# Side stages of a two-layer decoder step weighted anew, a store wait moved by one stage, and head groups regrouped

## The chip, the cores and the metric

The kernel runs on one core of one Trainium2 chip. The core has a matrix engine (PE, with its weight loads as PEld), a vector engine (DVE), a scalar engine (ACT), a general engine (POOL) and a sync engine (SP), and 16 DMA engines that move data between the chip's memory (HBM) and the on-chip SBUF. The metric is the device time of one execution in microseconds (us).

## The reference

It is one inference step of a decoder trunk with two layers, for a prompt of 256 tokens and 32 new tokens of eight running sequences ("samples"), 1024 wide, all in float32. Each layer has a mixer and then a PEER expert layer, each followed by `x <- LayerNorm(ALPHA * x + sublayer(x))`.

```
layer 0 mixer   HGRN2 recurrence (8 heads) beside sparse attention (8 query heads, 2 kv heads)
layer 1 mixer   q, k, v = x @ w_in (1024 x 3072), rotated; 16 heads of dilated attention,
                samples also over 256 cached positions each; o @ w_out (1024 x 1024)
expert layer    q = x @ w_q (1024 x 2048); scores against 2 x 128 sub-keys per head, 8 heads;
                top 16 of each half, top 16 of their sums -> 128 experts per token, softmax gate
                y = sum over the 128 of  gate * gelu(u[e] . x) * v[e]
```

Outputs are the new x of prompt and samples and the new cache rows, among them keys and values of layer 1 (`dil_p`, `dil_s`).

## The kernel before, in words

The tokens lie in three tiles: prompt tiles 0 and 1 of 128 tokens, and tile 2 with the 32 samples. The first mixer and the routing of tile 2 run alone, until about 650 us. Then one long block runs both expert layers as 576 **steps** (class `Experts`). A visit is one layer's experts for one tile; the visits are, in this order, layer 0 tiles 2, 0, 1 and layer 1 tiles 0, 1, 2, with 32, 128, 128, 128, 128 and 32 steps (`VISITS`, `FIRST`; four experts of each sample share a step). Step s does this:

- POOL fetches for each of the 128 partitions one expert row (u and v side by side, 8 KB) by an indirect DMA into a slot of the ring `uv`, which has 8 slots (L1802). It waits until step s - 8 has released the slot.
- DVE multiplies u with x and sums (`dot`, L1820). ACT makes gelu and the weight, and spreads the weight on a diagonal (L1866, L1875, L1888).
- PE adds diagonal times v into two banks of PSUM (L1912, three steps later), four matmul instructions a row. For steps that `by_dve` names, DVE does it instead: `acc += w * v` (L1834). `by_dve(s)` is true where s modulo 4 is in the third entry of the window in `WINDOWS` that holds s. At the end of a visit PE adds `acc` to its sum (L1919), and DVE forms the norm.

Beside the steps run **side stages**: the routing of the tile that comes next, and the layer 1 mixer of each tile. `WINDOWS` gives for each list of side stages the step at which it begins. A prompt tile's list (`dilated_tile`) is: transposes of x; the projection to q, k and v (`project_wide`, 12 weight pieces of 1 MB through 3 slots); `rotate_and_store` on DVE; `turn_qk` (transposes of q and k on PE); attention; output projection and norm; transposes; then the projection of the routing queries. The samples' list is split in two: `samples_first_part` runs in the window "samples" with head groups 0 and 1, `samples_second_part` in "mixer 2" with groups 2 and 3. A head group (`dilated_sample`) transposes 2 MB of cached keys, forms scores and sums 2 MB of cached values; SP fetches them by 16 DMAs of 256 KB, the first group's during the stage before it, the next group's keys and values when the group before has read its own.

Each engine runs one program. A stage is cut in ticks with a weight each, and `both` deals the ticks of a window to its steps so that the share of weight done follows the share of steps done. At the end of each stage the three engines drain and add to a semaphore `ended`; SP adds its own (L2015) after it has issued the stage's DMAs and the next stage's early loads, and nobody goes on before all four are there (L1948, L1951, L2018). A stage's end is thus a barrier for the expert steps too. `rotate_and_store` (L1445) ends on SP's side with a wait for all stores so far (`wait_for_stores`), and this keeps SP from adding.

```
weights = [0.5] * 2 + [w for st in stages for w in st.weights + [0.5] * 2] if stages else []
...
next(main)
while done < len(weights) and (n == b - a - 1 or reached[done] * (b - a) <= reached[-1] * (n + 1)):
    next(side)
    done += 1
```

Of the kernel before, what the change touches and what calls it, by code (L numbers as in the profile page):

```python
# [326 lines left out]
def transposes(k, name, groups, banks=ALL_BANKS, loads=(), early=False, after=(), by=("vector", "scalar")):  # L327

    nc, nb = k.nc, len(banks)
    turned, v_out, s_out, loaded = [k.sem(name, n) for n in ("turned", "v_out", "s_out", "loaded")]
    ident, n_by = k.c("ident"), len(by)
    stage = Stage(k, len(groups) + 1, 1.5)
    stage.read = [(turned, len(groups))]
    sizes = [(srcs[0].shape[0], int(np.prod(srcs[0].shape[1:]))) for srcs, _ in groups]
    copies = {"vector": (v_out, nc.vector.tensor_copy), "scalar": (s_out, nc.scalar.copy)}
    outs = [copies[engine] for engine in by]
    stage.done = [(outs[side][0], len(range(side, len(groups), n_by))) for side in range(n_by)]

    def out_view(i):
        (rows, width), (srcs, dst) = sizes[i], groups[i]
        flat = k.bank(banks[i % nb])[0:width, 0:rows * len(srcs)]
        if len(dst.shape) == 3:
            return flat.rearrange("p (a b) -> p a b", b=dst.shape[2])
        return flat

    @stage.on("early loads" if early else "sync")
    def _(sp):
        for dst, src in loads:  # L350
            sp.dma_start(dst, src).then_inc(loaded, 16)

    @stage.on("tensor")
    def _(pe):
        if loads:
            pe.wait_ge(loaded, 16 * len(loads))
        wait_all(pe, after)
        for i, (srcs, dst) in enumerate(groups):
            rows, width = sizes[i]
            j = i - nb  # L360
            if j >= 0:
                pe.wait_ge(outs[j % n_by][0], j // n_by + 1)
            for n, src in enumerate(srcs):
                last = nc.tensor.transpose(k.bank(banks[i % nb])[0:width, n * rows:(n + 1) * rows], src, ident[0:rows, 0:rows])
            last.then_inc(turned, 1)
            yield
        yield

    def take_out(eng, side):
        done, copy = outs[side]  # L370
        yield
        for i in range(len(groups)):
            if i % n_by == side:
                eng.wait_ge(turned, i + 1)
                copy(groups[i][1], out_view(i)).then_inc(done, 1)  # L375
            yield

    for side, engine in enumerate(by):
        stage.on(engine)(lambda eng, side=side: take_out(eng, side))
    return stage  # L380
# [83 lines left out]
def project_wide(k, name, w, groups, out, wbuf, t, banks, after=(), by=("vector", "scalar"), resident=False):  # L464
# [19 lines left out]
    for at, base, n_j, done in ends:  # L484
        for j in range(n_j):
            spot = min(at + j // 2, len(ticks) - 1)
            ticks[spot].append(("leave", base + j, done))
    stage = Stage(k, len(ticks), 1.0)
    n_by = len(by)
    copies = {"vector": (v_out, nc.vector.tensor_copy), "scalar": (s_out, nc.scalar.copy)}  # L490
    outs = [copies[engine] for engine in by]
# [143 lines left out]
def project_out_and_norm(k, name, catT, w_piece, gain, bias, w, gb, z, stats, tiles=(0, 1, 2), banks=ALL_BANKS, before_loads=(),  # L635
# [5 lines left out]
    row_landed, used, variance, rooted, normed = [k.sem(name, n) for n in ("rows_landed", "w_used", "variance", "rooted", "normed")]  # L641
    n_t, pieces = len(tiles), KC // 2
    per = [len(w_piece(i, w[:, 0])) for i in range(pieces)]
    stage = Stage(k, pieces * n_t * 2 + 3 * n_t, 1.2)
    stage.weights[pieces * n_t * 2:] = [3.5] * (3 * n_t)
    stage.tile_done = [[(normed, n + 1)] for n in range(n_t)]
    stage.rows_in = rows_in or (row_landed, 32)

# [96 lines left out]
def attention(k, name, items, bufs, pairs=(0, 2), turn_banks=(4, 5), before_scores=(), before_values=()):  # L745
# [18 lines left out]

    ticks = []

    def scores(i):
        if i < n_items:
            count = len(items[i]["scores"])
            for at in range(0, count, 3):  # L770
                ticks.append([("scores", i, at, min(at + 3, count))])
# [8 lines left out]
    for i in range(n_items):  # L780
# [9 lines left out]
                    ticks[-1] = [("turn", r + 1), ("copy", r + 1)] + ticks[-1]  # L790
        ticks.append([("leave", i)])
    stage = Stage(k, len(ticks), 1.0)
    stage.read = [(summed, len(rounds))]

    def view(i):
# [646 lines left out]
def rotate_and_store(k, name, qk, val, tiles, out_p, out_s, tmp):  # L1442

    nc = k.nc
    rotated = k.sem(name, "rotated")  # L1445
    stage = Stage(k, 4 * len(tiles), 2.5)

    @stage.on("vector")
    def _(dve):
        for n, t in enumerate(tiles):  # L1450
            r = ROWS[t]
            for at in (0, 512, 1024, 1536):
                rotate(k, qk[0:r, n, at:at + 512], qk[0:r, n, at:at + 512], (t, r), HEADS // 2, tmp)
                if at == 1536:
                    nc.vector.memset(k.pad[:, :], 0.0).then_inc(rotated, 1)
                yield

    @stage.on("sync")
    def _(sp):
        for n, t in enumerate(tiles):  # L1460
            sp.wait_ge(rotated, n + 1)
            dst = out_s[0].rearrange("b t x h d -> (b t) x (h d)") if t == 2 else \
                out_p[0, 0, 128 * t:128 * (t + 1)].rearrange("p x h d -> p x (h d)")
            k.store(sp, dst[:, 0, :], qk[0:ROWS[t], n, D:2 * D])
            k.store(sp, dst[:, 1, :], val[0:ROWS[t], t, :])
        k.wait_for_stores(sp)
    return stage


# [95 lines left out]
def route(k, name, layer, t, qT, keysT, slots, gate, xs, ctx, bank0, routed=None, own=None, after=()):  # L1565
# [26 lines left out]
    weights += [0.5, 0.5]  # L1592
    TICKS = len(weights)
    stage = Stage(k, TICKS, 1.0)
    stage.weights = weights

    def copy_out(copy, b):
        return copy(s[0:r, 4 * b:4 * b + 8].rearrange("p a b -> p (a b)"),
# [126 lines left out]
WINDOWS = (  # L1725
    ("route 0 0", FIRST[0], ()),
    ("route 0 1", FIRST[1] - 6, ()),
    ("samples", FIRST[1] + 42, (3,)),
    ("mixer 0", FIRST[2] + 6, (3,)),
    ("route 1 0", FIRST[3] - 48, ()),  # L1730
    ("nothing", FIRST[3] - 10, (3,)),
    ("mixer 1", FIRST[3] + 6, (3,)),
    ("route 1 1", FIRST[4] - 48, ()),
    ("mixer 2", FIRST[4] - 10, (3,)),
    ("route 1 2", FIRST[5] - 48, ()),
# [219 lines left out]
def experts_and_side_work(k, experts, windows):  # L1955

    ended = k.sem("side_stage_ended")
    spans = []
    for i in range(len(windows)):
        spans.append((windows[i][0], windows[i + 1][0] if i + 1 < len(windows) else experts.ticks))  # L1960

    def both(name, eng):
        main = {"tensor": experts.tensor, "vector": experts.vector, "scalar": experts.scalar}[name](eng)
        base = 0
        for (a, b), (_, stages) in zip(spans, windows):
            side = side_ticks(k, stages, name, eng, ended, base) if stages else iter(())
            weights = [0.5] * 2 + [w for st in stages for w in st.weights + [0.5] * 2] if stages else []
            base += len(stages) + 1 if stages else 0
            reached = np.cumsum(weights)
            done = 0  # L1970
            for n in range(b - a):
# [4 lines that stand above are left out]
            for _ in side:  # L1976
                raise AssertionError("side work left over")
        for _ in main:
            raise AssertionError("steps left over")

    with k.nc.Block() as block:
        @block.gpsimd
        def _(pool):
            experts.pool(pool)

        @block.tensor
        def _(pe):
            both("tensor", pe)

        @block.vector  # L1990
        def _(dve):
            both("vector", dve)

        @block.scalar
        def _(act):
            both("scalar", act)

        @block.sync
        def _(sp):
            experts.load_rows(sp, 0)  # L2000
            n, layer = 0, 1
            for start, stages in windows:
                if not stages:
                    continue
                if layer < DEPTH and start > FIRST[layer * TILES] + LAG + 2:
                    experts.load_rows(sp, layer)
                    layer += 1
                chain = [Stage(k, 0)] + stages
                for stage, following in zip(chain, stages + [None]):
                    if "sync" in stage.parts:  # L2010
                        stage.parts["sync"](sp)
                    if following and "early loads" in following.parts:
                        following.parts["early loads"](sp)
                    n += 1
                    sp.sem_inc(ended, 1)  # L2015
                    sp.wait_ge(ended, 4 * n)
                    for sem in stage.sems:
                        sp.sem_clear(sem)  # L2018
            experts.stores(sp)
# [36 lines left out]
def turn_qk(k, name, t, qk, qT, kT):  # L2056

    groups = [([qk[0:ROWS[t], 0, at + 128 * (c + j):at + 128 * (c + j + 1)] for j in range(4)], dst[:, c:c + 4, cols(t)])
              for dst, at in ((qT, 0), (kT, D)) for c in range(0, HP, 4)]
    return transposes(k, name + "_qk", groups, SIDE_BANKS)  # L2060


def mix_out(k, name, t, a, w, ctx, before_loads=()):
# [20 lines left out]
def samples_first_part(k, name, a, o, val, kT, qT, wbuf, cached):  # L2084
# [9 lines left out]
            stages.append(rotate_and_store(k, name + "_rot", qk, val, (2,), o["dil_p"], o["dil_s"], tmp))  # L2094
        stages.append(turn_qk(k, name, 2, qk, qT, kT))
    with ExitStack() as outer:
        stages += sample_groups(k, name, (0, 1), a, qT, kT, val, cached, outer)
    return stages


def samples_second_part(k, name, a, val, kT, qT, cached):
# [1 line left out]


    with ExitStack() as outer:
        stages = sample_groups(k, name, (2, 3), a, qT, kT, val, cached, outer)
        w = cached[:, 0].rearrange("p b n (c z) -> p (b n c) z", z=256).rearrange("p (s c n) z -> p s c (n z)", s=2, c=2)
        stages.append(mix_out(k, name, 2, a, w, outer, stages[-1].stages[0].read))
    stages.append(transpose_x(k, name + "_y", (2,), SIDE_BANKS))
# [174 lines left out]
```

## Time and profile before

| what | value |
|---|---|
| median of 3 runs | 2496.88 us (2495.08 to 2505.72) |
| profiled execution | 2510.64 us, its span 2508.9 us |
| mean granted PE clock | 0.856 of full speed |
| bytes moved | 750.84 MB, mean 299 GB/s |

The page gives for each engine its busy time as a share of the span, then the span in 40 equal slices (62.7 us each) with one digit per slice. The busy table of the trace gives the same for any stretch: length, then busy time and instruction count of PE, PEld, DVE, ACT and POOL, then the granted PE clock, the mean busy share of the 16 DMA engines, and GB/s. A share can read a little over 1, as transfers overlap at the edges. In lists of instructions the bracket gives how long the engine had been idle and what released it.

### The profile page before, as it was taken

What the parts mean: (1) busy time and instruction counts of PE and PEld (TensorE: products, weight loads), DVE (VectorE), ACT (ScalarE), POOL (GpSimd) and SP (SyncE); (2) the same over time, 40 slices, a digit from 0 to 9 for tenths busy, and PEclk for the clock granted to TensorE, in tenths of its full rate; (3) what the DMA queues carried; (4) which work ended last, traced back from release to release, by engine and by line L of the source; (5) the groups of instructions that cost most, each with busy time, mean ns of one, the idle gap of its engine ahead of it and who ended that gap; (6) DMA issues with size and microseconds to landing.
All of it is one profiled execution on the core that took longest, in us unless ns stands there. A gap on an engine that the chain in (4) does not pass through costs nothing. (4 is left out here: it accounts for less than half of the span.)

```text
span 2508.9 us, 19125 instructions
## 1 busy us (share of the span) xinstructions
PE 1942.4 (77%) x5651; PEld 886.6 (35%) x5651; DVE 1458.8 (58%) x3327; ACT 570.5 (23%) x1755; POOL 702.9 (28%) x612
## 2 busy tenths in 40 slices
PE   8968288899567797679867877767798687888675
PEld 3356155534213322344323432323343244323221
DVE  0043633138599846565376498548649766547975
ACT  0010122101223312222143223215222232212222
POOL 4000000000234523333133344323334333334442
PEclk9986556698789998887989998888899888899988
DMA  8300120300689999998989999987999999899997
GB/s 279 94 17 1 38 68 0 141 27 1 253 297 386 422 420 400 396 389 348 394 342 387 422 419 387 415 339 311 351 421 420 360 369 398 341 414 421 405 385 297
DMA packets 144945, 750.84 MB, mean 299 GB/s; under 512 B 22077, under 2 KB 46537, under 8 KB 63817
## 3 DMA queue, kind: packets, MB, share of 16 engines
q0 software_dynamic: 84480, 608.21, 60.1%
q1 hardware_dynamic: 60360, 141.41, 15.3%
q8 instruction: 45, 0.74, 0.1%
q14 instruction: 60, 0.48, 0.1%
HBM read 743.96 MB, written 5.60 MB: 299 GB/s over the span
## 5 line engine op out<-in xcount | busy, mean ns | idle before, releaser
L1912 PE MATMUL ps<-uv,diag 128*128 128x512 f32 (+1 forms) x1908 | 1013.6, 672 | 318.0 <-ACT diag L1888 206.7
L1802 POOL DMA_INDIRECT uv<-in_experts_dram,slots x576 | 672.3, 1167 | 1743.1 <-PE ps L1912 1051.8
L1820 DVE CUSTOM_DVE_ANT_0 uv<-uv,x 128x1024 f32<-128x1024 f32 x512 | 621.8, 1226 | 430.5 <-DMA uv<-in_experts_dram,slots 345.7
L1912 PEld LDWEIGHTS ps<-uv,diag 128*128 128x128 f32 (+1 forms) x1908 | 358.4, 201 | 876.5 <-issue 557.7
L1866 ACT ACTIVATE gelu<-dot 128x2 f32<-128x2 f32 x288 | 58.6, 203 | 1066.3 <-DVE dot L1820 1066.1
L1888 ACT ACTIVATE diag<-const,wgt 128x128 f32<-128x128 f32 (+1 forms) x477 | 166.5, 386 | 9.4
L1875 ACT ACTIVATE wgt<-gate,gelu 128x1 f32<-128x1 f32 x576 | 138.0, 287 | 68.0 <-PEq L1948 31.6
L1834 DVE SCALAR_TENSOR_TENSOR acc<-uv,wgt,acc 128x1024 f32<-128x1024 f32 x94 | 120.4, 1281 | 0.8 <-ACT wgt L1875 0.8
L441 PE MATMUL ps<-even_w,xT 128*128 128x512 f32 (+3 forms) x240 | 100.2, 570 | 6.6 <-issue 5.3
L1820 DVE CUSTOM_DVE_ANT_0 uv<-uv,xs 128x1024 f32<-128x1024 f32 x64 | 78.1, 1225 | 44.0 <-DMA uv<-in_experts_dram,slots 41.3
L524 PE MATMUL ps<-uv,xT 128*128 128x512 f32 (+1 forms) x192 | 85.9, 609 | 1.8 <-ACT xT L375 1.8
L524 PE MATMUL ps<-last_w,xT 128*128 128x512 f32 x160 | 76.3, 621 | 12.1 <-DMA last_w<-in_odd_w_in_dram 11.7
L524 PE MATMUL ps<-first_w,xT 128*128 128x512 f32 x160 | 73.1, 599 | 12.2 <-DMA first_w<-in_odd_w_in_dram 10.6
L441 PEld LDWEIGHTS ps<-even_w,xT 128*128 128x128 f32 (+1 forms) x240 | 38.1, 165 | 68.3 <-issue 64.2
L456 DVE COPY h<-ps 128x512 f32<-128x512 f32 (+3 forms) x8 | 5.0, 627 | 91.2 <-PE ps L441 51.6
L524 PEld LDWEIGHTS ps<-uv,xT 128*128 128x128 f32 (+1 forms) x192 | 32.2, 169 | 53.6 <-issue 51.1
L524 PEld LDWEIGHTS ps<-last_w,xT 128*128 128x128 f32 x160 | 31.0, 197 | 54.3 <-issue 36.2
L524 PEld LDWEIGHTS ps<-first_w,xT 128*128 128x128 f32 x160 | 29.6, 190 | 53.8 <-issue 33.2
L879 DVE TENSOR_TENSOR q_rows<-ps,const 128x512 f32<-128x512 f32 (+3 forms) x16 | 10.2, 640 | 63.7 <-PE ps L824 63.7
L1820 DVE DVE_READ_ACCUMULATOR2_ANT dot<- 128x1 f32 x576 | 47.2, 82 | 0.0
L524 PE MATMUL ps<-sample_w_in,xT 128*32 128x512 f32 x96 | 44.4, 596 | 2.7 <-DMA sample_w_in<-in_odd_w_in_dram 2.6
L1062 PE MATMUL ps<-hT,hg_key 64*128 64x128 f32 (+1 forms) x304 | 24.7, 317 | 22.4 <-PEq L1008 13.2
(430 smaller groups left out, 1930.8 us busy)
## 6 DMA issues: line engine op xcount, KB each, us to landing
sample_cache<-in_cache_dil_kv_dram SPq DMA_DIRECT2D x64, 256.0 KB
sample_w_in<-in_odd_w_in_dram SPq DMA_DIRECT2D x12, 1024.0 KB
first_w<-in_odd_w_in_dram SPq DMA_DIRECT2D x12, 1024.0 KB
last_w<-in_odd_w_in_dram SPq DMA_DIRECT2D x12, 1024.0 KB, 10.7
uv<-in_experts_dram,slots POOLq DMA_INDIRECT x576
even_w<-in_even_w_in_dram SPq DMA_DIRECT2D x8, 1024.0 KB, 8.4
uv<-in_peer_w_q_dram SPq DMA_DIRECT2D x8, 1024.0 KB, 13.9
first_w<-in_peer_w_q_dram SPq DMA_DIRECT2D x8, 1024.0 KB, 10.4
```

Source lines behind the costliest of these rows:

```text
L441: last = nc.tensor.matmul(k.bank(banks[i % nb])[0:ROWS[t], 0:widths[j]], k.xT[:, 4 * half + c, cols(t)], wbuf[:, load % slots, c, 0:widths ...
L456: copy(out(j, t), k.bank(banks[i % nb])[0:ROWS[t], 0:widths[j]]).then_inc(done, 1)
L524: last = nc.tensor.matmul(k.bank(banks[job])[0:r, :], k.xT[:, chunk, cols(t)], wbuf[:, i % slots, width * c + 512 * j:width * c + 512 * (j ...
L879: step(nc.vector.tensor_tensor(view(i), sc, bc(it["mask"], 1, g), ALU.add))
L1062: last = nc.tensor.matmul(dst, key[p, hd // 2, cols(t)], pT[p, hd // 2, cols(t)], start=True, stop=True, skip_group_check=True)
L1802: self.k.nc.gpsimd.indirect_dma_start(out=self.uv[:, s % RING, :], out_offset=None, in_=self.table, in_offset=bass.IndirectOffsetOnAxis(ap ...
L1820: ins = nc.vector.tensor_tensor_reduce(self.uv[:, s % RING, 0:D], self.uv[:, s % RING, 0:D], x, 1.0, 0.0, ALU.mult, ALU.add, self.dot[:, g ...
L1834: nc.vector.scalar_tensor_tensor(self.acc[:, :], v, w, self.acc[:, :], ALU.mult, ALU.add).then_inc(self.added, 1)
L1866: nc.scalar.activation(self.gelu[:, grp % 2, :], self.dot[:, grp % 2, :], ACT.Gelu).then_inc(self.gelued, 1)
L1875: ins = nc.scalar.activation(self.wgt[:, grp % 2, g:g + 1], self.gate[:, t, j:j + 1], ACT.Copy, scale=self.gelu[:, grp % 2, g:g + 1])
L1888: last = nc.scalar.activation(self.diag[:, step % RING, 0:w], k.c(shape), ACT.Copy, scale=self.wgt[:, grp % 2, g:g + 1])
L1912: last = nc.tensor.matmul(k.bank(c)[0:m, :], self.diag[:, s % RING, 0:m], self.uv[:, s % RING, D + 512 * c:D + 512 * (c + 1)], start=(j == ...
```

## The change

It does six things. The weights of the ticks are set anew: transposes 0.9 for 1.5, projection 1.9 for 1.0 (its last tick 0.8), output projection 1.9 for 1.2 and its three norm ticks 3.6, 1.6 and 3.1 for 3.5 each, rotation 3.0 for 2.5, route ticks times 2.5 (alone in their windows, so only their ratio to the ends of stages changes), ends of stages 0.3 for 0.5 (two ticks each). Attention ticks get a weight each from a function of what the tick does. The wait for the stores moves from the rotation to the stage after it, `turn_qk`, ahead of that stage's early loads. Head group 2 moves from "mixer 2" to "samples". The window "samples" begins 4 steps earlier. In the windows "samples", "mixer 0" and "mixer 1" DVE adds every second row and not every fourth.

```diff
@@ transposes
-    stage = Stage(k, len(groups) + 1, 1.5)
+    stage = Stage(k, len(groups) + 1, 0.9)
@@ project_wide
-    stage = Stage(k, len(ticks), 1.0)
+    stage = Stage(k, len(ticks), 1.9)
+    stage.weights[-1] = 0.8
@@ project_out_and_norm
-    stage = Stage(k, pieces * n_t * 2 + 3 * n_t, 1.2)
-    stage.weights[pieces * n_t * 2:] = [3.5] * (3 * n_t)
+    stage = Stage(k, pieces * n_t * 2 + 3 * n_t, 1.9)
+    stage.weights[pieces * n_t * 2:] = [3.6, 1.6, 3.1] * n_t
@@ attention
+    def work(tick):
+        pe = dve = 0.2
+        for what, at, *some in tick:
+            it = items[rounds[at][0] if what in ("turn", "copy", "values") else at]
+            sweep = it["groups"] * it["n"] / 840
+            if what == "scores":
+                pe += 0.4 * (some[1] - some[0])
+            elif what == "turn":
+                pe += 0.2 * it["groups"]
+            elif what == "values":
+                pe += (0.36 if it["groups"] == 1 else 0.18) * (some[1] - some[0])
+            elif what == "mask":
+                dve += 2 * sweep
+            elif what == "normalise":
+                dve += (1 if it["count"] is None else 3) * sweep + 0.2
+            elif what == "leave":
+                dve += 0.2
+        return max(pe, 1.2 * dve)
...
     stage = Stage(k, len(ticks), 1.0)
+    stage.weights = [work(tick) for tick in ticks]
@@ rotate_and_store
-    stage = Stage(k, 4 * len(tiles), 2.5)
+    stage = Stage(k, 4 * len(tiles), 3.0)
...
-        k.wait_for_stores(sp)
     return stage
@@ route
-    stage.weights = weights
+    stage.weights = [2.5 * w for w in weights]
@@ WINDOWS
-    ("samples", FIRST[1] + 42, (3,)),
-    ("mixer 0", FIRST[2] + 6, (3,)),
+    ("samples", FIRST[1] + 38, (1, 3)),
+    ("mixer 0", FIRST[2] + 6, (1, 3)),
...
-    ("mixer 1", FIRST[3] + 6, (3,)),
+    ("mixer 1", FIRST[3] + 6, (1, 3)),
@@ experts_and_side_work
-            weights = [0.5] * 2 + [w for st in stages for w in st.weights + [0.5] * 2] if stages else []
+            weights = [0.3] * 2 + [w for st in stages for w in st.weights + [0.3] * 2] if stages else []
@@ turn_qk
-    return transposes(k, name + "_qk", groups, SIDE_BANKS)
+    stage = transposes(k, name + "_qk", groups, SIDE_BANKS)
+
+    @stage.on("sync")
+    def _(sp):
+        k.wait_for_stores(sp)
+    return stage
@@ samples_first_part
-        stages += sample_groups(k, name, (0, 1), a, qT, kT, val, cached, outer)
+        stages += sample_groups(k, name, (0, 1, 2), a, qT, kT, val, cached, outer)
@@ samples_second_part
-        stages = sample_groups(k, name, (2, 3), a, qT, kT, val, cached, outer)
+        stages = sample_groups(k, name, (3,), a, qT, kT, val, cached, outer)
```

## Rows read from the trace of the kernel before

**Rows 1.** Page, part 1: busy time of each engine, share of the span, instructions.
```profile
PE 1942.4 (77%) x5651; PEld 886.6 (35%) x5651; DVE 1458.8 (58%) x3327; ACT 570.5 (23%) x1755; POOL 702.9 (28%) x612
```
**Rows 2.** Page, part 2: DMA busy tenths and GB/s in 40 slices.
```profile
DMA  8300120300689999998989999987999999899997
GB/s 279 94 17 1 38 68 0 141 27 1 253 297 386 422 420 400 396 389 348 394 342 387 422 419 387 415 339 311 351 421 420 360 369 398 341 414 421 405 385 297
```
**Rows 3.** Page, part 3: DMA queues with packets, MB, share of 16 engines.
```profile
q0 software_dynamic: 84480, 608.21, 60.1%
q1 hardware_dynamic: 60360, 141.41, 15.3%
```
**Rows 4.** Busy table, last stretch without side work.
```profile
2389.00:2492.00 103.00, 72.02 (x131) 19.53 (x132) 67.65 (x103) 26.66 (x97) 45.39 (x38) 0.85 0.97 397
```
**Rows 5.** Busy table: two head groups; mixer 0 projection, rotation, turning, attention.
```profile
1019.50:1097.30 77.80, 60.08 (x219) 31.21 (x219) 45.69 (x75) 20.91 (x67) 28.02 (x25) 0.87 1.01 399
1097.30:1173.50 76.20, 71.45 (x223) 38.79 (x223) 51.49 (x85) 23.27 (x68) 28.36 (x24) 0.79 0.88 350
1182.90:1252.60 69.70, 58.41 (x132) 24.49 (x132) 21.59 (x32) 10.21 (x34) 14.33 (x14) 1.00 0.97 398
1252.60:1277.20 24.60, 9.11 (x20) 3.63 (x20) 16.96 (x38) 3.55 (x13) 6.79 (x6) 0.79 0.84 328
1277.20:1286.10 8.90, 8.62 (x28) 4.44 (x28) 7.15 (x11) 3.63 (x11) 3.97 (x3) 0.83 0.39 133
1286.10:1332.70 46.60, 35.01 (x125) 15.62 (x125) 40.23 (x72) 27.24 (x64) 18.40 (x15) 0.85 1.01 417
```
**Rows 6.** Busy table: mixer 1 projection to attention; mixer 2 groups, output projection.
```profile
1595.20:1670.90 75.70, 62.25 (x132) 26.19 (x132) 21.23 (x32) 9.99 (x34) 13.12 (x14) 0.91 0.93 376
1670.90:1695.10 24.20, 9.20 (x16) 3.37 (x16) 15.80 (x36) 2.67 (x10) 6.23 (x5) 0.68 0.89 327
1695.10:1705.30 10.20, 10.05 (x29) 5.29 (x30) 7.83 (x12) 3.52 (x11) 3.08 (x4) 0.75 0.44 148
1705.30:1772.50 67.20, 46.51 (x180) 22.58 (x178) 51.59 (x74) 31.51 (x71) 21.02 (x17) 0.82 0.84 329
1994.30:2068.30 74.00, 65.58 (x216) 36.00 (x217) 48.40 (x81) 22.28 (x63) 24.44 (x22) 0.80 0.96 362
2068.30:2141.70 73.40, 60.65 (x211) 31.54 (x210) 39.76 (x67) 19.15 (x60) 24.83 (x23) 0.85 0.94 374
2141.70:2190.30 48.60, 37.02 (x76) 11.54 (x76) 29.20 (x44) 12.30 (x38) 18.00 (x16) 0.89 0.92 356
```
**Rows 7.** Instructions in order of time, end of mixer 0's rotation (start, length, instruction).
```profile
1270.02 0.36 SPq L177 DMA_DIRECT2D out_dil_p_dram<-first_qk  x1
...
1277.31 3.44 PE L1912 MATMUL ps<-uv,diag 128*128 128x512 f32 x4 [13.57 <-SPq L2018]
1277.35 1.23 DVE L1820 CUSTOM_DVE_ANT_0 uv<-uv,x 128x1024 f32<-128x1024 f32 x1 [7.35 <-SPq L2018]
```
**Rows 8.** Groups of DVE instructions by line, mixer 1 attention: busy, mean ns.
```profile
L1820 DVE CUSTOM_DVE_ANT_0 uv<-uv,x 128x1024 f32<-128x1024 f32 x17 | 20.2, 1222 | 0.4 <-ACT gelu L1866 0.2
L1834 DVE SCALAR_TENSOR_TENSOR acc<-uv,wgt,acc 128x1024 f32<-128x1024 f32 x4 | 5.1, 1280 | 0.0
```
**Rows 9.** Instructions in order of time, PE, end of mixer 0's projection.
```profile
1241.22 3.70 PE L524 MATMUL ps<-first_w,xT 128*128 128x512 f32 x8 [1.79 <-DMA first_w<-in_odd_w_in_dram]
1244.76 1.88 PE L1912 MATMUL ps<-uv,diag 128*128 128x512 f32 x4
```
**Rows 10.** Instructions in order of time, SP's cache loads in the samples window.
```profile
992.38 5.18 SPq L351 DMA_DIRECT2D sample_cache<-in_cache_dil_kv_dram  x8
997.60 21.78 SPq L1525 DMA_DIRECT2D sample_cache<-in_cache_dil_kv_dram  x8
1041.18 16.21 SPq L351 DMA_DIRECT2D sample_cache<-in_cache_dil_kv_dram  x8
```
**Rows 11.** Busy table of SP's filter, the steps stopped behind cache loads: clock, DMA, GB/s.
```profile
1990.00:2000.00 10.00, 0.50 1.03 330
```

## The prediction

> **What bounds the kernel now.** I read the page's engine shares and slices first, then the DMA queues, then the busy table stage by stage, then the instructions in order of time at the stage ends. On the whole span nothing looks full: PE 77%, DVE 58% [rows 1]. The slices tell more: from the 14th on, when the expert steps run, the DMA engines are nine tenths busy nearly everywhere, and where they are, they move 420 to 422 GB/s [rows 2]. The rows that the expert steps fetch are 608 of 751 MB [rows 3]. One step fetches 128 x 8 KB = 1.05 MB; at 421 GB/s that is 2.49 us. The stretch without side work that ends the kernel has DMA at 0.97 with PE and DVE at 0.70 and 0.66 of its 103 us [rows 4]. So the time of the 576 steps is bytes over 421 GB/s plus what the DMA engines stand idle. The change moves no byte: it can only take idle DMA time away or add some.
>
> Where is that idle time? One minus the DMA share, times the length, from the busy table: last head group of the samples window 9.1 us; mixer 0, projection 2.1, rotation 3.9, turning 5.4; mixer 1, projection 5.3, rotation 2.7, turning 5.7, attention 10.8; mixer 2, head groups 3.0 and 4.4, output projection 3.9 [rows 5, 6]. Together 56 us. (A full stretch reads 1.01, so this is a little low.)
>
> **The change, part by part.** A stage gets its share of its window's steps by weight. I worked the weight lists out with both sets of numbers; the old ones give 16.7 steps for mixer 1's attention, where the trace has 17 dots [rows 8]. Steps before -> after: samples projection 20.8 -> 25.4, rotation 8.8 -> 6.8, turning 6.8 -> 2.8, head group 25.2 -> 19.7 (and there are three). Mixer 0: projection 13.5 -> 20.0, rotation and turning 10.1 -> 7.6, attention 15.0 -> 15.2, output 10.9 -> 10.3. Mixer 1: projection 13.1 -> 17.8, rotation and turning 9.9 -> 6.7, attention 16.7 -> 21.7, output 10.7 -> 9.1. Mixer 2: one head group of 30.8 steps for two of 22.6, output 15.1 -> 20.4. The steps whose row DVE adds up rise from 99 to 160 (every second instead of every fourth in three windows).
>
> *The store wait.* At the end of each rotation SP waits until the keys and values are stored before it lets the three engines on. In mixer 0 it issued the stores at 1270.0 and PE and DVE ran again at 1277.3: DVE had waited 7.35 us, PE 13.57 [rows 7]. PE stood still, released no ring slot, and the DMA share fell to 0.84 and 0.39. Moved behind the turning (2 to 3 steps, some 6 us), the wait is nearly over when SP comes to it. Gone: 3.9 + 5.4 + 2.7 + 5.7 = 17.7 us. In the samples window DMA was not idle there, so nothing is counted. What is late next is DVE. Mixer 0, 7.6 steps: 7.6 dots x 1.22, 3.8 additions x 1.28 [rows 8] and the stage's own 16.96 - 6 x 1.22 - 1.28 = 8.4, with about 1.0 of copies, make 23.6 us, against 7.6 x 2.49 + 2.5 for the stores = 21.4 us of DMA. Mixer 1 by the same sum: 21.9 against 19.2. Left idle: 5. Net -12.7.
>
> *The projections.* Eight projection matmuls take 3.54 us from start to start at the granted clock of 1.00, so one is 0.44 and a step's row (four) 1.77 [rows 9]. In mixer 0 after: 96 x 0.44 + 10 x 1.77 = 60 us of PE, against (20.0 x 1.05 + 12.6)/0.421 = 80 us of DMA. PE no longer follows weights that have just landed. The 2.1 + 5.3 us go but for 0.5: -6.9.
>
> *The attention.* In mixer 1 DVE was busy 51.6 of 67.2 us (77%); 17 dots and 4 additions are 25.8, so the attention itself is 25.8. After: 21.7 x 1.22 + 10.9 x 1.28 + 25.8 = 66 us, against 21.7 x 2.49 + 7.5 (three weight pieces) = 61.5 of DMA. DVE bounds this stage. At 90% busy it takes 73.5, 12 over; the ring of eight rows takes up some 3 of it. I keep 9 of the old 10.8: -1.8. In mixer 0 the same sum gives 43.8 of DVE against 45.3, at 90% 3.4 over: +2. Bounds: none over, and 24.7 over in mixer 1 if DVE stays at 77%.
>
> *The third head group.* A group after: PE 60.1 us at clock 0.87 is 52 at full clock, 19 rows x 1.77 of it the steps' own, so 19 of its own [rows 5]; with 9.9 rows on PE 36 us, against (19.7 x 1.05 + 4.2)/0.421 = 59 of DMA. It fits. The last group still ends where the visit ends; I keep 5 of 9.1: -4.1. Mixer 2 loses a group and has room: 11.3 -> 1.3, -10.0.
>
> *The rest* (transposes at 0.9, norm ticks, the 0.3 around a stage, the route window) moves ticks by less than two steps between stages where DMA already reads about 1.01 [rows 5]: 0, bounds -3 and +3.
>
> Sum: -12.7 - 6.9 - 1.8 + 2 - 4.1 - 10.0 = -33.5. The profiled execution took 2510.6 (span 2508.9 and 1.7 around it), so 2477 in its terms; it ran 13.8 above the median of the runs. Against 2496.9 I forecast 2463.
>
> **Rivals.** *DVE is the new bound.* DVE takes 61 more additions, 61 x 1.28 = 78 us. If its stages keep their old busy share (77% in mixer 1, 86% in mixer 0), attention gives 24.7 and 5.5 over, and rotation with turning 9.2 each, which eats the store gain: -6.9 - 10.0 - 4.1 + 0.7 + 13.9 + 5.5 = -0.9, 2496. For it: DVE waited in mixer 1 though not full. Against: more steps per tick are more room between its waits.
>
> *All idle time goes*: -56, 2441. For it: each stage but two fits with room. Against: the end of a visit has idle time that no weight removes.
>
> *SP is held by its queue* (slower). In the samples window SP issues 16 cache loads during the turning, after the change behind the store wait. With the queue empty eight issues took 5.18 us, 0.65 each; the next eight took 21.78, and a later eight 16.21 [rows 10]: if four and five of them were quick, the others took 4.8 and 4.3 each. In 2.8 steps they don't fit: the engines wait at the stage's end. If 11 of the 16 took 5 us, the stage would take 5 x 0.5 + 55 + 5 = 62 us, while the DMA engines have 16 x 0.26 + 8 x 1.05 = 12.6 MB, 30 us: 32 idle, and 8 more at each of two group ends: 48 - 33.5 = +14.5, 2511. Against: with the rows stopped the loads alone kept DMA at 1.03 and 330 GB/s [rows 11], so the queue drains when the ring is full. It decides if that speed is not reached. The Trainium skill (DMA: Bandwidth & Descriptors, Queues, rings and completion order) says that an engine takes turns between queues packet by packet; the small cache packets then get a small share beside 8 KB rows and the full one without them, which the two issue rates here agree with.
>
> *The PE clock falls* (slower). With fewer rows PE idles more. The granted clock was 1.00 where PE was busy 58.4 of 69.7 us and 0.68 to 0.87 in the patchier stages, and a row's four matmuls took 3.44 us at the low level against 1.88 [rows 5 to 7, 9]. If groups and output projections ran wholly at 1.2 GHz: a group 72 us of PE against 59, 13 x 3 = 39 over; outputs (32 x 0.44 + 5.2 x 1.77 = 23 at full clock, 22 in mixer 1) 46 against 31 and 44 against 28, 31 over: 70 - 33.5 = +36.5, 2533. It decides when their clock goes below about 0.65; it was 0.79 to 0.99. The Trainium skill (TensorE: Matmul & The Clock Gate, HAM oscillation) warns of just this, PE gaps behind DMA waits throttling each burst; the row after the 13.57 us gap, at the low level, agrees.
>
> **How the numbers follow.** Forecast 0.55 (2450 to 2480), all idle gone 0.12, DVE bound 0.18, SP 0.08, clock 0.07. Half a per cent is 12.5 us, about what this kernel's measurement can tell. Faster: 0.67 and 0.03 of the DVE case, 0.70. Same: 0.13 of DVE's, 0.03 of SP's, 0.01 of the clock's, 0.17. Slower: 0.13. The range leaves out SP's and the clock's cases and the extreme of full removal: 2436 to 2503.
>
> **What would show it.** The rotation-to-turning passage of mixers 0 and 1 at DMA 0.9 or more, with PE and DVE not released by SP; projections at 1.00; the DVE wait for rows present in the group stages; attention of mixer 1 with DVE 0.85 to 0.95 busy. It is wrong if the DMA share of attention falls below 0.8, if SP's 16 issues in the samples window leave DMA below 0.9, or if PEclk there is under 0.7.

## The result and the profile after

| | before | after |
|---|---|---|
| median of the runs | 2495.98 us (4 runs) | 2470.78 us (4 runs, 2458.0 to 2471.85) |
| ratio | 1 | 0.9879, 95% interval 0.9838 to 0.992 |
| profiled execution | 2510.64 us, span 2508.9 | 2469.82 us, span 2468.0 |
| mean granted PE clock | 0.856 | 0.841 |

The forecast was 2463 us, 33.5 us less than before, in a range of 2436 to 2503. The medians lie 25 us apart and the means 30 (2498.0 and 2467.9); the ratio stands for 30 us less (20 to 40). All ratios below leave out executions in the chip's slower state, one of which, of the kernel "rows to DVE only, PE's matmuls put back", took 4597 us. First the page of the kernel after, parts 1 and 2 as in [rows 1, 2].

```profile
PE 1848.0 (75%) x5407; PEld 851.8 (35%) x5407; DVE 1529.8 (62%) x3388; ACT 553.8 (22%) x1694; POOL 721.3 (29%) x612
DMA  8300120300588999999999999999899999999997
GB/s 282 97 18 1 38 69 0 135 35 1 211 334 344 421 420 392 356 370 375 415 403 373 405 415 420 404 413 359 312 369 412 420 373 419 411 421 421 416 382 304
```

PE lost 94 us of busy time and DVE gained 71: the 61 additions of 1.28 us are 78, and the rest of DVE's work took 7 less. Neither says where time was won. The DMA line does: from the 14th to the 39th slice five digits were under 9 before, and one is after. The bytes are the same (750.8 MB).

Now the busy table of the kernel after by stage (length; busy time of PE, PEld, DVE, ACT, POOL; clock, DMA share, GB/s). In order: the samples' turning and three head groups; mixer 0's projection, rotation, turning, attention.

```profile
976.30:1000.20 23.90, 9.21 (x24) 4.20 (x24) 6.54 (x10) 1.60 (x7) 3.75 (x4) 0.57 0.93 336
1000.20:1066.80 66.60, 51.78 (x179) 31.36 (x179) 41.65 (x66) 15.93 (x49) 21.16 (x18) 0.68 0.94 346
1066.80:1131.30 64.50, 46.02 (x183) 26.03 (x183) 42.95 (x68) 16.31 (x50) 24.27 (x20) 0.79 1.01 392
1131.30:1187.80 56.50, 45.55 (x187) 26.04 (x187) 47.09 (x76) 18.53 (x50) 19.99 (x20) 0.89 0.95 368
1195.00:1270.50 75.50, 64.37 (x136) 26.94 (x136) 38.28 (x53) 12.29 (x43) 22.74 (x22) 0.93 1.01 419
1270.50:1289.00 18.50, 10.69 (x12) 3.22 (x12) 17.81 (x38) 3.06 (x11) 5.94 (x5) 0.63 1.01 399
1289.00:1301.80 12.80, 5.35 (x20) 4.03 (x20) 6.40 (x10) 2.46 (x7) 3.52 (x3) 0.78 0.98 355
1301.80:1347.40 45.60, 28.18 (x108) 13.60 (x108) 42.35 (x73) 25.78 (x59) 15.23 (x14) 0.80 0.98 380
```

Mixer 1's projection, rotation, turning, attention and output projection; mixer 2's head group and output projection.

```profile
1593.40:1674.40 81.00, 64.38 (x136) 26.79 (x136) 34.73 (x48) 11.20 (x39) 18.32 (x18) 0.94 1.00 408
1674.40:1691.70 17.30, 4.41 (x8) 1.36 (x8) 16.68 (x36) 3.06 (x11) 6.56 (x6) 0.71 0.86 321
1691.70:1699.30 7.60, 5.48 (x20) 3.69 (x20) 5.45 (x9) 2.14 (x6) 2.11 (x2) 0.75 0.76 263
1699.30:1776.10 76.80, 48.72 (x172) 23.44 (x172) 64.92 (x89) 31.96 (x73) 24.16 (x22) 0.76 0.86 340
1776.10:1811.30 35.20, 22.82 (x48) 9.53 (x48) 21.74 (x32) 7.99 (x22) 11.18 (x10) 0.91 0.88 346
1986.80:2070.50 83.70, 71.57 (x243) 35.95 (x243) 60.78 (x99) 27.00 (x81) 38.96 (x31) 0.93 0.99 394
2070.50:2130.40 59.90, 44.39 (x92) 14.15 (x92) 36.63 (x55) 14.96 (x48) 24.16 (x21) 0.94 1.01 416
```

Read with one minus the DMA share, times the length, as in the prediction:

| idle DMA time, us | before | forecast | after |
|---|---|---|---|
| rotation and turning, mixers 0 and 1 | 17.7 | 5 | 4.5 |
| projections, mixers 0 and 1 | 7.4 | 0.5 | 0 |
| mixer 1 attention | 10.8 | 9 | 10.8 |
| mixer 0 attention | 0 | 2 | 0.9 |
| head groups of the samples window | 9.1 | 5 | 6.8 |
| mixer 2, groups and output projection | 11.3 | 1.3 | 0.8 |
| not in the forecast: mixer 1 output projection (1776.1) | 0.3 | - | 4.2 |
| not in the forecast: samples' turning | 0.5 | - | 1.7 |

(Before, the samples' turning, 992.4 to 1019.5 us, had DMA at 0.98.) The forecast stages fall from 56.3 to 23.8 us, 32.5 less, against 33.5 forecast; the two at the bottom take 5.1 back, which leaves 27.4. The two spans lie 41 us apart, but 4.5 of it lies ahead of the first fetch of the expert steps (650.7 and 646.2 us), in a part that the change doesn't touch, and the profiled execution before was above the median by 14 us, so I don't count all of it as the change's.

### The profile page after: what moved, and what is told of

Same layout as the page of the kernel before. It is cut to its first block, busy times and chain, and to the rows that moved or that the text cites. A ratio compares the mean times of both kernels' runs of the same rounds, so it can differ in the third digit from the quotient of the medians.

```text
span 2468.0 us, 18705 instructions
## 1 busy us (share of the span) xinstructions
PE 1848.0 (75%) x5407; PEld 851.8 (35%) x5407; DVE 1529.8 (62%) x3388; ACT 553.8 (22%) x1694; POOL 721.3 (29%) x612
## 4 chain that ended last, share of the span: by engine, by line
DMA 22%; DVE 20%; PE 18%; issue 5%; SPq 1%; ACT 1%; POOL 1%; PEldq 1%; DVEq 1%; PEld 0%; ACTq 0%
DMA uv<-in_experts_dram,slots 14%; PE ps L1933 9%; DVE uv L1841 7%; PE ps L525 4%; DVE acc L1855 2%; DMA last_w<-in_odd_w_in_dram 2%; DMA first_w<-in_odd_w_in_dram 2%; PE ps L846 1%; PE ps L685 1%; SPq L1546 1%; PE ps L874 1%; DVE route_s L1675 1%; DMA out_dil_p_dram<-dil_val 1%; DMA last_w<-in_peer_w_q_dram 1%; DMA sample_rows<-in_peer_sub_keys_dram 1%
## 5 line engine op out<-in xcount | busy, mean ns | idle before, releaser
L1823 POOL DMA_INDIRECT uv<-in_experts_dram,slots x576 | 690.7, 1199 | 1685.2 <-PE ps L1933 923.2
L1933 PE MATMUL ps<-uv,diag 128*128 128x512 f32 (+1 forms) x1664 | 897.1, 681 | 286.5 <-ACT diag L1909 222.1
L1933 PEld LDWEIGHTS ps<-uv,diag 128*128 128x128 f32 (+1 forms) x1664 | 314.2, 202 | 783.4 <-issue 446.7
L1855 DVE SCALAR_TENSOR_TENSOR acc<-uv,wgt,acc 128x1024 f32<-128x1024 f32 x155 | 198.4, 1280 | 2.0 <-ACT wgt L1896 2.0
L1909 ACT ACTIVATE diag<-const,wgt 128x128 f32<-128x128 f32 (+1 forms) x416 | 148.7, 386 | 9.4
L685 PE MATMUL ps<-even_w_out,xT 128*128 128x512 f32 (+1 forms) x96 | 42.8, 607 | 0.0
## 6 DMA issues: line engine op xcount, KB each, us to landing
uv<-in_peer_w_q_dram SPq DMA_DIRECT2D x8, 1024.0 KB, 13.9
```

Of the source, the lines that this page charges most:

```text
L685: last = nc.tensor.matmul(bank(n, h)[0:ROWS[t], :], catT[:, 2 * i + c, cols(t)], w[:, i % slots, c, 512 * h:512 * (h + 1)], start=(i == 0 ...
L1823: self.k.nc.gpsimd.indirect_dma_start(out=self.uv[:, s % RING, :], out_offset=None, in_=self.table, in_offset=bass.IndirectOffsetOnAxis(ap ...
L1855: nc.vector.scalar_tensor_tensor(self.acc[:, :], v, w, self.acc[:, :], ALU.mult, ALU.add).then_inc(self.added, 1)
L1909: last = nc.scalar.activation(self.diag[:, step % RING, 0:w], k.c(shape), ACT.Copy, scale=self.wgt[:, grp % 2, g:g + 1])
L1933: last = nc.tensor.matmul(k.bank(c)[0:m, :], self.diag[:, s % RING, 0:m], self.uv[:, s % RING, D + 512 * c:D + 512 * (c + 1)], start=(j == ...
```

## The experiments

All ratios are to the kernel before, which ran beside the kernel tested on the same chip. There were three such sets of four kernels, each on a chip of its own, in the order of the table. The medians of the kernel before were 2495.2, 2496.9 and 2490.6 us, and two ratios of one set compare better than two of different sets. They are told in the order in which they answer.

| kernel | ratio | interval |
|---|---|---|
| store wait moved, nothing else | 0.9959 | 0.9923 to 0.9996 |
| weights only | 0.9934 | 0.9908 to 0.996 |
| rows to DVE only | 1.0048 | 1.0018 to 1.0077 |
| regrouping only | 1.0025 | 0.9997 to 1.0053 |
| after, store wait put back | 0.9925 | 0.9898 to 0.9953 |
| after, DVE rows as before | 0.9859 | 0.9818 to 0.9901 |
| after, groups two and two | 0.9899 | 0.9872 to 0.9926 |
| after, store wait later still | 0.9877 | 0.9848 to 0.9906 |
| rows to DVE only, PE's matmuls put back | 1.0027 | 1.0 to 1.0055 |
| after, PE's matmuls put back | 0.9976 | 0.9949 to 1.0002 |
| after, wait later, DVE rows as before | 0.9893 | 0.9852 to 0.9934 |
| after, wait later, DVE rows as before in mixer 1 | 0.9872 | 0.9837 to 0.9907 |

**The store wait, alone and taken back.**

```diff
 def rotate_and_store        # store_only: before with
-        k.wait_for_stores(sp)
 def turn_qk                 # the wait as its "sync" part
+        k.wait_for_stores(sp)
```

> The kernel before with only the store wait moved from the rotation to the turning stage. Theory (the time is bytes over 421 GB/s plus idle DMA time, and the wait costs what DMA idles in rotation and turning of the two prompt mixers): 17.7 us of idle there, some 4 stay because DVE is a little over in the rotation, so about -13 us, ratio 0.995; in the samples window nothing, since DMA was busy there. Rival (the ring makes up for the wait later): within 3 us of before. Rival (SP is held: the cache loads of the samples window now stand behind the stores): slower by up to 5 us, and the engines wait longer than 9 us at the end of the samples' turning.

> The kernel after with the store wait back at the end of the rotation. Theory: as in the kernel before, rotation and turning of both prompt mixers idle the DMA engines for some 18 us where the kernel after has 4: about 12 us slower than the kernel after, ratio to the kernel before 0.993. Rival (the turning of the kernel after is too short to hide the wait, as its engines still waited 6.3 us there in mixer 0): 5 us slower than after at most, 0.990.

Alone it is worth 0.41%, 10 us; taken out of the kernel after it costs 0.46%, 11.5 us, though the intervals of those two overlap and they come from different sets. The theory said 13 and 12. The busy table of the first, mixer 0's rotation and turning, then mixer 1's, and of the second, the same four stages:

```profile
1240.90:1259.20 18.30, 10.81 (x20) 4.22 (x20) 16.94 (x38) 3.55 (x13) 6.69 (x6) 0.82 0.95 370
1259.20:1268.30 9.10, 8.88 (x28) 4.44 (x28) 7.15 (x11) 3.64 (x11) 3.97 (x3) 0.80 0.92 339
1653.10:1670.30 17.20, 9.19 (x16) 3.37 (x16) 15.78 (x36) 2.67 (x10) 6.24 (x5) 0.76 0.97 364
1670.30:1680.80 10.50, 10.27 (x29) 5.34 (x30) 7.86 (x12) 3.53 (x11) 3.12 (x4) 0.74 0.83 304
```

```profile
1257.70:1283.80 26.10, 7.91 (x12) 2.32 (x12) 19.42 (x40) 3.25 (x12) 7.97 (x7) 0.69 1.01 418
1283.80:1289.90 6.10, 5.65 (x20) 4.19 (x20) 4.77 (x7) 2.26 (x6) 0.06 (x1) 0.66 0.07 28
1667.80:1693.80 26.00, 5.57 (x8) 1.85 (x8) 17.17 (x37) 3.06 (x11) 6.07 (x6) 0.68 0.82 300
1693.80:1700.10 6.30, 5.48 (x20) 3.69 (x20) 3.92 (x6) 1.26 (x3) 0.94 (x1) 0.70 0.00 0
```

With the wait the rotation lasts 24 to 26 us, and in the kernel after the turning behind it has next to no DMA (0.07 and 0.00): the rows asked for had landed while the engines stood still, and POOL asked for the next one only when PE had released a slot, 10.8 and 15.7 us after its last request. Without the wait the rotation lasts 17 to 18 us and DMA stays at 0.83 or more. So in these stages the ring doesn't make up for the wait. As a whole the interval of the first run still reaches 0.9996, within the 3 us of that rival; it is the table that speaks against it. The third theory, SP held in the samples window, came in part: at the end of the samples' turning PE now waited 17.7 us for 13.9, but with DMA at 1.03, so it cost nothing that shows.

**The weights alone.** The kernel after with the wait, the third entries and the groups as before.

> The kernel after with the store wait, the third entries of the windows and the head groups as before, so that only the weights of the ticks are new. Theory: the projections' 7.4 us of idle time go, mixer 2's output projection has 3.9 of which 2 go, the attention gets more steps but DVE has one row in four only, so 4 of its 10.8 go; the turning is shorter, which leaves the store wait as it was: about -13 us, ratio 0.995. Rival (the weights only shift the idle time from stage to stage): within 4 us of before.

Measured 0.9934, 16.5 us, the largest gain of the four parts. The reverse, the kernel after with the old weights, was not run. Its busy table: mixer 0's projection, mixer 1's attention, mixer 2's output projection.

```profile
1163.30:1242.00 78.70, 70.10 (x156) 29.71 (x156) 32.37 (x48) 13.73 (x48) 23.49 (x21) 0.98 1.01 419
1693.10:1763.70 70.60, 49.84 (x196) 23.56 (x194) 60.47 (x86) 34.20 (x81) 25.77 (x22) 0.90 0.95 369
2117.00:2165.60 48.60, 37.89 (x76) 10.96 (x76) 29.23 (x44) 11.73 (x36) 19.73 (x16) 0.89 1.01 411
```

Against [rows 5, 6] DMA goes from 0.97 to 1.01, from 0.84 to 0.95 and from 0.92 to 1.01. The attention lasts 3.4 us longer and takes five steps more.

**The rows alone, and with PE's load put back.**

```diff
-    ("samples", FIRST[1] + 42, (3,)),        # rows_only: before with (1, 3) in three windows
+    ("samples", FIRST[1] + 42, (1, 3)),
...
+                elif s % 4 == 1:             # rows_warm: in Experts.tensor, zeros x constant
+                    for c in range(2):
+                        nc.tensor.matmul(k.bank(c)[0:m, :], self.zero[:, 0:m], k.const[:, 0:512], start=False, stop=False,
+                                         skip_group_check=True)
```

> The kernel before with only the third entries of the windows samples, mixer 0 and mixer 1 set to (1, 3), so that DVE adds every second row there. Theory: PE sets the pace at the ends of the projections (idle 2.1 and 5.3 us), in part of mixer 1's attention and in the last head group (9.1); half of that goes, about -9 us, ratio 0.996. Rival (DVE is the new bound): mixer 1's attention gains DVE work of 4 x 1.28 = 5 us and the rotations 3 in all, which cancels it: 0. Rival (the PE clock falls with fewer rows): clock in the head groups from 0.87 and 0.79 to under 0.7 and the time up by 5 us or more.

> rows_only with PE's load put back without DVE's taken away: for the rows that moved to DVE (steps with s modulo 4 = 1) PE adds a tile of zeros times a constant tile, so PE issues the same matmuls as the kernel before and DVE the same additions as rows_only. If the loss of rows_only (1.0048) comes from the PE clock, which fell from 0.99 to 0.87 and 0.85 in the two output projections, the clock comes back and this is as fast as before, 1.000, the output projections at 3 us of excess over their bytes, not 6. If it comes from DVE's additions, this stays at 1.005. If PE's relief was worth something all the same, it is slower than both, 1.008.

My theory of 9 us gained was wrong: the part is a loss, 1.0048. The output projections of mixers 0 and 1 tell of the clock. In the busy table, as they were before, where [rows 5, 6] left them out:

```profile
1332.70:1370.10 37.40, 28.45 (x64) 11.75 (x64) 21.93 (x33) 9.07 (x26) 15.73 (x12) 0.99 0.98 386
1772.50:1806.60 34.10, 28.53 (x64) 11.83 (x64) 22.99 (x35) 9.17 (x27) 16.02 (x12) 0.99 0.99 382
```

With the rows alone:

```profile
1322.60:1363.80 41.20, 26.05 (x52) 10.54 (x52) 25.16 (x37) 8.20 (x23) 14.86 (x12) 0.87 0.93 361
1765.30:1805.30 40.00, 28.90 (x56) 11.59 (x56) 26.64 (x38) 8.29 (x24) 13.87 (x13) 0.85 0.90 353
```

With PE's matmuls put back:

```profile
1327.80:1366.10 38.30, 30.00 (x64) 12.10 (x64) 24.18 (x35) 8.20 (x23) 15.40 (x12) 0.95 0.89 348
1775.60:1814.30 38.70, 30.23 (x64) 12.42 (x64) 26.47 (x38) 8.29 (x24) 15.25 (x12) 0.93 0.93 360
```

In mixer 1 PE has 8 matmuls fewer than before (56 for 64) and is busy as long (28.90 against 28.53): what the rows gave, the clock took, 0.85 for 0.99. Put back, the clock rises to 0.93 to 0.95, the DMA share doesn't. As a whole 1.0027 lies between the two theories, and its interval touches 1.0 and overlaps that of the rows alone (from another set). What can be said: with the weights of before, the extra matmuls on PE cost nothing that can be measured, so taking them off was worth nothing measurable. In the two output projections the clock came back and the idle DMA time did not (6.9 us in both kernels, 1.1 before), which speaks for DVE there. How the whole loss is split between clock and DVE stays open.

**The regrouping alone, and taken back.** Head groups (0, 1, 2) and (3,) with the window begun at `FIRST[1] + 38`, in the kernel before; and (0, 1) and (2, 3) with `+ 42` in the kernel after.

> The kernel before with only head group 2 moved to the samples window and that window begun 4 steps earlier, weights as before: groups of 20.6 steps (three) and one of 30 in mixer 2. Theory: mixer 2's idle time (11.3 us in groups and output projection) falls to 3, the samples window's rises by 4 because the projection there gets 17 steps for 20.8: about -4 us, ratio 0.998. Rival (SP is held by its queue at three group ends in the samples window): +5 us or more.

> The kernel after with two head groups early and two late, and the samples window begun at step 74 again. Theory: mixer 2 is back at two groups in 66% of its steps and its idle time rises from 9 to some 20 us over its bytes; the samples window has two groups with more room and loses 10 of its 28: together 0 to +5 against after, ratio to before 0.989. Rival (the regrouping is what makes the four parts worth more together than alone): 10 us slower than after, 0.992.

Alone it is no gain (1.0025); I had expected one. Its last early group, where the visit ends:

```profile
1126.10:1191.60 65.50, 58.59 (x207) 32.42 (x207) 42.88 (x73) 20.92 (x59) 21.31 (x18) 0.84 0.81 314
```

DMA at 0.81 is 12.4 us idle, where before had 9.1 [rows 5]. In mixer 2 the regrouping alone did what was forecast: its head group (2025.0 to 2106.2 us) and output projection (2106.2 to 2164.0) had DMA at 0.99 and 1.00, 0.8 us idle for 11.3. These two places make 7 us of gain, and the runs show none; what took it back was not found. Taken out of the kernel after, the regrouping costs 0.2%, which the intervals can't tell from nothing.

**The rows in the kernel after.**

> The kernel after with every third entry (3,) again: DVE adds one row in four. If the 61 more additions hurt here as they did alone (rows_only 1.0048), this is 10 us faster than the kernel after, ratio to before 0.984; the attention of mixer 1 shows 8 to 9 us of excess over its bytes, not 14.8, as weights_only did. Rival (with three groups in the samples window PE needs the relief, and the four parts together gave 0.9879 where their single ratios multiply to 0.9966): slower than the kernel after by 10 us, 0.992, with the lost time in the three head groups.

> The same on the kernel after: PE's matmuls as in after_rows3, DVE's additions as in the kernel after. Mixer 1's attention tells the causes apart: 14.8 us of excess over its bytes in the kernel after, 7.6 in after_rows3, at clocks 0.76 and 0.90. Clock theory: the clock goes back to about 0.9 and the excess to 8 to 10. DVE theory: the excess stays at 14 to 17. Time: clock theory 0.986, DVE theory 0.988 to 0.992 of before.

Mixer 1's attention, then the first and the last early head group, with (3,) everywhere, and below with PE's matmuls put back and DVE's additions kept:

```profile
1710.30:1779.10 68.80, 49.86 (x192) 23.32 (x192) 59.20 (x84) 33.31 (x78) 22.80 (x22) 0.90 0.95 374
994.90:1059.60 64.70, 48.28 (x199) 27.18 (x199) 36.86 (x62) 17.26 (x54) 23.55 (x19) 0.90 0.94 369
1124.20:1183.70 59.50, 53.84 (x207) 29.79 (x207) 41.22 (x71) 19.61 (x54) 24.22 (x19) 0.91 0.92 339
```

```profile
1714.80:1789.40 74.60, 52.39 (x195) 24.64 (x193) 65.73 (x91) 32.62 (x76) 26.84 (x22) 0.86 0.88 352
999.70:1070.60 70.90, 55.42 (x199) 30.46 (x199) 41.41 (x66) 15.80 (x49) 21.09 (x18) 0.81 0.88 327
1134.90:1195.10 60.20, 53.56 (x207) 29.79 (x207) 47.28 (x76) 18.46 (x50) 20.88 (x20) 0.91 0.92 339
```

The same matmuls, without and with 61 more additions on DVE: 0.9859 against 0.9976, intervals apart. So the additions cost 1.2%, 29 us. The two are of different sets; against the nearest kernel of its own set (wait later, DVE rows as before, 0.9893) it is 0.8%. The attention shows 5.8 us of it (68.8 to 74.6 us, with 21 and 22 dots), at clocks 0.90 and 0.86, and the first head group 6.2 (64.7 to 70.9 us); where the rest lies was not looked for. The same additions, with and without the matmuls: 0.9976 against 0.9879, intervals apart, so here taking rows off PE wins 1.0% back. Both theories had this kernel at 0.992 or less; both were too low. The two effects cancel: the part as a whole is 0.9879 against 0.9859, nothing that can be measured. In the attention of the kernel after the clock is 0.76, PE is busy 48.7 us against 49.9 with (3,) though it has 20 matmuls fewer, and DMA is at 0.86. The idle DMA time there is 3.4 us with (3,), 9.0 with the additions and all matmuls, 10.8 in the kernel after: most of it came with the additions, little when the matmuls were taken off and the clock fell.

**A later wait, and the two mixed.** In the kernel after, engines still waited 6.5 to 7.5 us at the end of mixer 0's turning: SP issued the stores only at 1288.1, and the stage was 2 steps long. In order of time:

```profile
1288.05 0.36 SPq L177 DMA_DIRECT2D out_dil_p_dram<-first_qk  x1
...
1289.04 3.51 PE L364 MATMUL ps<-const,first_qk 128*128 128x128 f32 x16 [3.00 <-SPq L2036]
1301.87 1.23 PE L846 MATMUL ps<-dil_kT,first_qT 64*128 64x128 f32 x8 [7.48 <-SPq L2036]
```

```diff
+            @stages[-1].on("sync")          # after dilated_prompt, ahead of the w_out loads
+            def _(sp):
+                k.wait_for_stores(sp)
...
+        def loads_then_wait(sp):            # samples: first head group's early loads, then the wait
+            loads(sp)
+            k.wait_for_stores(sp)
```

> The kernel after with the store wait later still: in the prompt mixers SP waits at the start of the attention, ahead of its weight loads, where no engine stands behind it; in the samples window after it has issued the 16 cache loads. Theory: the waits at the end of the turning go (6.3 us in mixer 0, 1.5 in mixer 1, and of the 17.6 in the samples window the 5 of the store), worth what DMA idled there: -4 us, ratio to before 0.986. Rival (the ring covers them already): no difference from after, 0.988.

> after_late with every third entry (3,): the weights, the three early groups and the later store wait, without the rows moved to DVE. after_rows3 had 0.9859 and after_late 0.9877 against 0.9879 of the kernel after; if both count, 0.984 to 0.986, the fastest so far. If the store wait was covered already, 0.986.

> after_late with (3,) in the window mixer 1 only, where DVE sets the pace of the attention: its excess goes from 16.2 to about 8 us, while mixer 0 and the samples window, where after_rows3 had 4 us more than the kernel after in mixer 0's attention and 4 more in the queries behind it, keep (1, 3). Theory: 5 us faster than after_late, 0.985. Rival (mixer 1's projection loses with (3,) what its attention wins, 5.3 against 2.4 us of excess): 0.987.

0.9877: no difference from the kernel after, though the 4 us of the theory (0.986) lie inside the interval as well. The turning of mixer 0 shrank, from 12.80 to 6.60 us, but DMA had been busy there:

```profile
1276.70:1283.30 6.60, 5.24 (x20) 3.94 (x20) 6.42 (x10) 2.46 (x7) 1.95 (x2) 0.75 0.96 338
```

A wait that holds the engines and not the DMA engines costs nothing here that can be measured. (3,) everywhere on top gave 0.9893, (3,) in mixer 1 alone 0.9872. In the latter the attention had DMA at 0.94 in 71.1 us, 4.3 us idle for 10.8, as hoped; yet none of the three is told apart from the kernel after, and where the gain of the attention went is open. The best so far are four kernels between 0.9859 and 0.9879 with overlapping intervals.

## Why the prediction was right

**The frame held for the difference.** Time followed idle DMA time: 32.5 us less of it in the forecast stages, 27.4 with the two that were not forecast, and 30 us less time. For the level it did not hold. Over the whole block (first fetch to 17 us before the end) the busy table gives 1841 us at 385 GB/s before and 1805 at 393 after, some 709 MB each; at 421 GB/s that is 1684 us, and the idle share of 0.04 and 0.02 adds about 74 and 36. Some 80 us are left in both (roughly, as 0.01 of the share is 18 us), in which the DMA engines were busy and moved less than 421 GB/s, as they did when nearly all traffic was cache loads (330 GB/s at a share of 1.03 [rows 11]). The prediction took 421 for all slices where they are nine tenths busy, but such slices go down to 351 [rows 2]. The term stayed about the same and so fell out of the difference, which the prediction had assumed without saying so.

**The store wait** was forecast at -12.7; the two runs give -10 and -11.5, and the table 17.7 to 4.5. The 4.5 are nearly all in mixer 1, whose rotation and turning stayed at 0.86 and 0.76, below the 0.9 that was to show the forecast, while the sum had split the rest evenly (2.2 and 2.7). In mixer 0 SP still released PE and DVE, after 7.5 and 6.5 us, but with DMA at 0.98. **The projections** went to 1.01 and 1.00 as said. **Mixer 2** gave 10.5 for 10.0. For 3.9 of it the regrouping was not needed: the output projection went to 1.01 by the weights alone.

**What was mis-sized.** The attention of mixer 1: I had taken 1.8 us off, for 90% DVE; DVE was 64.9 of 76.8 us, 85%, for the forecast 66 us of work, and the idle time stayed at 10.8. The output projection behind it, at "0" in my rest, idled 4.2 us with 9 steps for 11. The samples window with three groups: idle 6.8 for the forecast 5, and 1.7 in the turning ahead of it. What the sum got right in total hides that two of its parts, rows and regrouping, are worth nothing measurable. I had booked -4.1 and -10.0 to the regrouping, and counted the rows' relief of PE in the projections (10 rows where 15 would have been; with the 15, weights alone, mixer 0's projection was at 1.01 too). That the total came out so near is partly luck. The four single ratios multiply to 0.9966, 8 us, where the whole gave 30, so the parts don't add up. Alone, the rows cost 12 us and the regrouping 6 (its interval starts at 0.9997), but together, on top of the new weights, nothing that can be measured (0.9925 against 0.9934). Why the new weights make them free is open. The product of weights and store wait alone, 0.9934 x 0.9959 = 0.9893, lies inside the interval of the whole; a kernel with these two only was not run.

**The rivals.** *DVE is the new bound* was half right: the additions do cost 0.8 to 1.2% at equal PE load, so the price was real, but PE's relief pays it back. *The PE clock falls*: it did in the first early head group (0.68 for 0.87), in mixer 0, and in mixer 1's attention and output projection. Nine of the stages above lie between 0.57 and 0.80, but some were as low before (mixer 1's turning 0.75 for 0.75), and in mixer 2 the clock rose (0.93 and 0.94 for 0.80 to 0.89). With that, one of the prediction's own signs of being wrong came true, a clock under 0.7 in the samples window (0.57 and 0.68), and the time was still as forecast: the sign was set too tight. The Trainium skill's rule (TensorE: Matmul & The Clock Gate, HAM oscillation) was right about the direction. No loss of time by it shows where DMA set the pace: the second group ran at 0.79 with DMA at 1.01, and the first had DMA at 0.94 both at a clock of 0.68 and, with (3,), at 0.90. In mixer 1's attention a clock of 0.86 for 0.76 went with DMA at 0.88 for 0.86. *SP is held*: at the end of the samples' turning PE waited 14.7 us, DVE 15.7 and ACT 16.6, but the 16 issues took 18.1 us in place of the 57.5 of the rival, with DMA at 0.93 over the stage. They are, in order of time:

```profile
981.95 10.41 SPq L351 DMA_DIRECT2D sample_cache<-in_cache_dil_kv_dram  x8
992.41 7.69 SPq L1546 DMA_DIRECT2D sample_cache<-in_cache_dil_kv_dram  x8
```

As [rows 11] had shown, the queue drains once the rows stop: POOL's last fetch here began at 987.70, ahead of the second eight. The store wait ahead of them is the gap from the stage's start at 976.3 to 981.95. A slip in the forecast's range: it says that it leaves out the full removal of idle time, 2441, but 2436 to 2503 holds it.

## What to carry to other kernels

Find the resource that is busy nearly everywhere, and cost each edit by the idle time that it takes from that resource: the store wait, 13.6 us of PE's time in mixer 0, was worth 5 to 6 a mixer, and one of 7.5 us nothing that could be measured, by what the DMA engines did meanwhile. Take the parts of a change apart even where the whole came out as forecast; here two of four carried it, and one of the others costs time by itself. Moving work off a matrix engine that waits anyway may only lower its clock; measure it with the other parts in place, as the same move was worth nothing with the old weights and 1.0% with the new.

## What the runs showed of the hardware

- Fewer matmuls did not mean less busy time: 56 matmuls took 28.90 us at a granted clock of 0.85 where 64 had taken 28.53 at 0.99.
- After a wait in which all fetched rows had landed, no transfer ran for the whole following stage (DMA 0.00 over 6.3 us), though PE was busy for 5.5 of it: POOL's next fetch had waited 15.7 us for PE to release a slot.
- SP's time to issue hangs on the traffic of the other queue: eight cache loads took 21.78 us beside flowing rows [rows 10], 10.41 beside the last four fetches and 7.69 when no further rows were asked for.
- The DMA engines can be busy throughout and move less: 330 GB/s at a share of 1.03 with nearly all traffic cache loads [rows 11], against 419 at 1.01 in mixer 0's projection.
